# Prompt attention of a hybrid decoder step: turned weights ahead of the next scores, mask and maximum in one VectorE pass, alternating score banks, outputs turned in threes

## The reference, cut to what matters

```python
# branch A, group g: s = q_g . k * HEAD_DIM**-0.5, masked to its band; p = exp(s - m); l = sum(p)
o = jnp.einsum('nbhqk,nbkhd->nbqhd', p / l, vc)
lse = m + jnp.log(l)
# merged: alpha = softmax(lse over the 3 groups); out = sum_g alpha_g * o_g
# branch B: s masked to the selected keys, p = softmax(s), o = p @ v
```

## Time and profile before

| | us |
|---|---|
| median of 3 runs | 3498.6 |
| profiled execution | 3499.64 |
| its span | 3498.1 |
| prompt attention, first score product to the end of the last output copy | 2163.5 to 2583.9 |
| TensorE busy over the span | 3278.1 (94%) |
| VectorE / ScalarE / GpSimd busy | 1736.3 / 742.1 / 250.3 |

### The profile page before, as it was taken

How to read it: one execution, slowest core, us unless ns; L and a number is a source line. 1 busy time by engine, 2 the same in 40 slices (tenths; PEclk the granted TensorE clock), 3 DMA queues, 4 the chain that set the end, 5 groups by cost and what they waited for, 6 DMA issues and landing times.

```text
span 3498.1 us, 52866 instructions
## 1 busy us (share of the span) xinstructions
PE 3278.1 (94%) x20840; PEld 3042.7 (87%) x20840; DVE 1736.3 (50%) x2497; ACT 742.1 (21%) x1166; POOL 250.3 (7%) x393
## 2 busy tenths in 40 slices
PE   6888999999999999999999997888988899999997
PEld 4656999999999999999999996566665699999997
DVE  4554878710332455554555553654433364564654
ACT  4121000011001112111111112222222233433332
POOL 3000000000000000000000000211113201000000
PEclk7889999999999999999999998999998899999998
DMA  9722222222222222332333327412037667495672
GB/s 322 240 86 87 73 68 74 74 73 62 67 73 61 80 85 87 91 108 69 99 96 91 101 64 230 122 49 66 13 99 240 209 213 211 140 279 140 194 208 78
DMA packets 522864, 422.04 MB, mean 121 GB/s; under 512 B 19835, under 2 KB 491131, under 8 KB 519491
## 3 DMA queue, kind: packets, MB, share of 16 engines
q1 hardware_dynamic: 500044, 338.53, 33.9%
q0 software_dynamic: 22720, 82.20, 6.3%
HBM read 346.96 MB, written 75.81 MB: 121 GB/s over the span
## 4 chain that ended last, share of the span: by engine, by line
PE 86%; DVE 5%; DMA 4%; ACT 2%; issue 1%; SPq 1%; POOL 0%; DVEq 0%; POOLq 0%; ACTq 0%
PE banks L278 18%; PE banks L280 18%; PE banks L279 18%; PE banks L1451 6%; PE banks L1453 6%; PE banks L1452 6%; PE banks L651 4%; DVE mx L574 2%; DMA ada_w<-in_w_ada 1%; PE banks L680 1%; PE banks L670 1%; PE banks L654 1%; DMA u_raw<-in_w_out 1%; PE banks L333 1%; PE banks L1991 1%
## 5 line engine op out<-in xcount | busy, mean ns | idle before, releaser
L278 PE MATMUL banks<-h_hi,w_hi 128*128 128x352 f32 (+2 forms) x3744 | 1227.0, 328 | 12.2 <-DVE w_lo L269 10.1
L280 PE MATMUL banks<-h_hi,w_lo 128*128 128x352 f32 (+2 forms) x3744 | 1222.3, 326 | 0.0
L279 PE MATMUL banks<-h_lo,w_hi 128*128 128x352 f32 (+2 forms) x3744 | 1221.4, 326 | 0.0
L278 PEld LDWEIGHTS banks<-h_hi,w_hi 128*128 128x128 f32 (+1 forms) x3744 | 701.6, 187 | 17.0 <-issue 15.7
L279 PEld LDWEIGHTS banks<-h_lo,w_hi 128*128 128x128 f32 (+1 forms) x3744 | 704.0, 188 | 1.3
L280 PEld LDWEIGHTS banks<-h_hi,w_lo 128*128 128x128 f32 (+1 forms) x3744 | 700.8, 187 | 1.3
L269 DVE TENSOR_TENSOR w_lo<-w_raw,w_hi 128x2048 fp32r<-128x2048 f32 (+1 forms) x79 | 180.0, 2278 | 640.7 <-ACT w_hi L265 532.0
L1501 DVE MAX8 best<-work 128x8 f32<-128x1088 f32 x224 | 289.3, 1291 | 10.8 <-issue 1.0
L304 ACT ACTIVATE col<-banks 128x384 f32<-128x384 f32 x150 | 71.2, 475 | 1027.6 <-PE banks L280 1027.6
L1503 DVE MATCH_REPLACE8 work<-best,work 128x1088 f32<-128x1088 f32 x224 | 285.8, 1276 | 0.0
L265 ACT CAST w_hi<-w_raw 128x2048 fp32r<-128x2048 f32 (+1 forms) x79 | 149.8, 1896 | 582.9 <-PE banks L280 538.7
(11 more groups left out here) (237 smaller groups left out, 3359.9 us busy)
## 6 DMA issues: line engine op xcount, KB each, us to landing
w_raw<-in_w_in SPq DMA_DIRECT2D x78, 1024.0 KB, 5.7
u_raw<-in_w_out SPq DMA_DIRECT2D x96, 512.0 KB, 5.4
scratch_proj<-col POOLq DMA_DIRECT2D x78, 544.0 KB, 3.0
ada_w<-in_w_ada SPq DMA_DIRECT2D x16, 2048.0 KB, 13.8
u_raw<-in_w_pb SPq DMA_DIRECT2D x48, 512.0 KB, 4.7
gate_w<-in_w_ada SPq DMA_DIRECT2D x16, 1024.0 KB, 7.7
u_raw<-in_w_pa SPq DMA_DIRECT2D x48, 256.0 KB, 3.2
gates<-scratch_proj SPq DMA_DIRECT2D x64, 192.0 KB, 2.5
```

Source lines behind the costliest of these rows:

```text
L278: nc.tensor.matmul(dst, w_hi[:, par, k, 0:width], h_hi[:, k, a:b], start=(k == 0), stop=False)
L279: nc.tensor.matmul(dst, w_hi[:, par, k, 0:width], h_lo[:, k, a:b], start=False, stop=False)
L280: mm = nc.tensor.matmul(dst, w_lo[:, par, k, 0:width], h_hi[:, k, a:b], start=False, stop=(k == KT - 1))
```

## The change

In the scores of A jobs in rows 4 to 7 (16 jobs) and of B jobs in rows 2 to 7 (48 jobs), called `in_place`, TensorE no longer adds the mask. VectorE reads scores and bf16 mask, adds them, multiplies by -SCALE, writes the result back to the same PSUM columns and accumulates the minimum straight into `nmx`, in one instruction; the exp then uses scale -1. The other 32 jobs keep mask product, maximum and multiplication.

TensorE's step n becomes: half 0 of job n-2, every third step the outputs of the last complete triple, scores of job n, half 1 of job n-2, values of job n-3. VectorE's step n becomes: copy of half 0 of job n-2, output copies, mask and maximum of job n, reciprocal and scaling of job n-3. ScalarE copies half 1 of job n-2 ahead of the exp of job n. Score banks go by triples: (0-3, 4-5, 0-1), then (2-5, 0-1, 4-5), so that the scores of a job share banks with the job two before, never with the one before. The outputs of a triple are turned as soon as its three jobs are scaled, in the free columns of bank 7. GpSimd's sums are cut anew: in rows 0 to 3 as before; in rows 4 to 7 blocks i-4 to 3 first, then blocks 4 to i, then the two near blocks. From row 5 on, half 0 of an A job waits only for the first of them.

```diff
-        s_bank = lambda n: 0 if JOBS[n][0] == "A" else 4 + (JOBS[n][2] % 2 if JOBS[n][1] < 4 else 0)
+        s_bank = lambda n: ((0, 4, 0), (2, 0, 4))[n // 3 % 2][n % 3]
+        in_place = lambda n: JOBS[n][1] >= (4 if JOBS[n][0] == "A" else 2)
...
+        triple_due = lambda n: (n - 4) // 3 if n >= 4 and (n - 4) % 3 == 2 else None
+        def group_sums(n):
+            i = JOBS[n][1]
+            near = (i - 1 if i else 0, i + 1, (i + 1 + min(5, i + 1)))
+            if i < 4:
+                return [(0, i + 1, i + 1), near]
+            return [(i - 4, 4, i + 1), (4, i + 1, i + 1 + 8 - i), near]
...
-            for n in range(NJ + 5):
-                if n < NJ:
-                    dve.wait_ge(s_done, n + 1)
-                    nc.vector.tensor_reduce(mx[:, n:n + 1], flat(s_bank(n), P, width_of(n)), AX, ALU.max)\
-                        .then_inc(mx_set, 1)
+            for n in range(NJ + 4):
                 m = n - 2
                 if 0 <= m < NJ:
                     dve.wait_ge(t_done, use_no["w", m, 0] + 1)
                     need(dve, pv_done, m - 1)
                     w = min(4, blocks_of(m)) * P
                     nc.vector.tensor_copy(p_t[:, m % 2, 0:w], banks[:, T_BANK, 0:w]).then_inc(t_out, 1)
...
+                    dve.wait_ge(ot_done, x + 1)
+                    nc.vector.tensor_copy(o_t[:, i % 2, a, :], banks[:, O_BANK, P:2 * P])
+                    nc.vector.tensor_copy(o_t[:, i % 2, HA + 2 * a:HA + 2 * a + 2, :], ...).then_inc(ot_out, 1)
+                if n < NJ:
+                    if in_place(n):
+                        nc.vector.tensor_tensor_reduce(out=src, in0=src, in1=mask, scale=-SCALE, scalar=-TAKEN,
+                                                       op0=ALU.add, op1=ALU.min, accum_out=nmx[:, n:n + 1])\
+                            .then_inc(nmx_set, 1)
...
+                    early = half == 0 and JOBS[n][1] >= 5
+                    pe.wait_ge(groups_added, sums_before(n) + (1 if early else len(group_sums(n))))
...
+            def turn_outputs(x):
+                i, a = x // HA, x % HA
+                pe.wait_ge(o_out, 3 * x + 3)
+                for y, m in enumerate((a, HA + 2 * a, HA + 2 * a + 1)):
+                    tr = nc.tensor.transpose(banks[:, O_BANK, (y + 1) * P:(y + 2) * P],
+                                             o_tok[:, i % 2, m * P:(m + 1) * P], ident[:])
+                tr.then_inc(ot_done, 1)
...
-            for n in range(NJ + 5):
+            for n in range(NJ + 4):
+                if 2 <= n < NJ + 2:
+                    turn_weights(n - 2, 0)
+                if triple_due(n) is not None:
+                    turn_outputs(triple_due(n))
                 if n < NJ:
                     scores(n)
-                if 2 <= n < NJ + 2:
-                    turn_weights(n - 2, 0)
+                if ("w", n - 2, 1) in use_no:
+                    turn_weights(n - 2, 1)
                 if 3 <= n < NJ + 3:
                     values(n - 3)
```

More of the change, by code:

```diff
@@ L421, in decode_step @@
         width_of = lambda n: (sum(s[1] for s in SEG(JOBS[n][1])) if JOBS[n][0] == "A" else JOBS[n][1] + 1) * P
-        s_bank = lambda n: 0 if JOBS[n][0] == "A" else 4 + (JOBS[n][2] % 2 if JOBS[n][1] < 4 else 0)
+        s_bank = lambda n: ((0, 4, 0), (2, 0, 4))[n // 3 % 2][n % 3]
+        in_place = lambda n: JOBS[n][1] >= (4 if JOBS[n][0] == "A" else 2)
         s_banks = lambda n: set(range(s_bank(n), s_bank(n) + (width_of(n) + 511) // 512))
         exps_before = lambda n: max([m + 1 for m in range(n) if s_banks(m) & s_banks(n)], default=0)
-        a_jobs = lambda n: sum(JOBS[m][0] == "A" for m in range(n))
         T_BANK, O_BANK = 6, 7
         USES = []
-        for n in range(NJ + 5):
-            if 2 <= n < NJ + 2:
[L432 to L436, removed]
-        use_no = {u: x for x, u in enumerate(USES)}
+        for n in range(2, NJ + 2):
+            USES.append(("w", n - 2, 0))
+            if blocks_of(n - 2) > 4:
+                USES.append(("w", n - 2, 1))
+        use_no = {u: x for x, u in enumerate(USES)}
+        triple_due = lambda n: (n - 4) // 3 if n >= 4 and (n - 4) % 3 == 2 else None
[5 more added lines that the diff above has]
+            return [(i - 4, 4, i + 1), (4, i + 1, i + 1 + 8 - i), near]
+        sums_before = lambda n: sum(len(group_sums(m)) for m in range(n) if JOBS[m][0] == "A")
         def flat(bank, rows, width):
@@ L512, in act_attention @@
             nc.scalar.copy(mask_b[:], mask_f[:]).then_inc(mask_cast, 1)
-            for n in range(NJ + 5):
+            for n in range(NJ + 2):
+                m = n - 2
+                if ("w", m, 1) in use_no:
+                    act.wait_ge(t_done, use_no["w", m, 1] + 1)
+                    nc.scalar.copy(p_t[:, m % 2, 512:blocks_of(m) * P], banks[:, T_BANK, 0:(blocks_of(m) - 4) * P]).then_inc(t_out, 1)
                 if n < NJ:
@@ L517, in act_attention @@
                     nc.scalar.activation(p_buf[n % 3][:, 0:width_of(n)], flat(s_bank(n), P, width_of(n)), ACT.Exp,
[L518 to L523, removed]
+                                         bias=nmx[:, n:n + 1], scale=-1.0 if in_place(n) else SCALE,
+                                         accum_out=lsum[:, n:n + 1]).then_inc(exp_done, 1)
             act_sample(act)
@@ L543, in pool_attention @@
                     pool.wait_ge(exp_done, n + 1)
[L544 to L548, removed]
+                    done = sums_before(n)
+                    for first, end, src in group_sums(n):
+                        dst = p_buf[n % 3][:, first * P:end * P]
+                        if src > i + 1 and end == i + 1 and first >= i - 1:
+                            pool.wait_ge(groups_added, done)
+                        nc.gpsimd.tensor_tensor(dst, dst, p_buf[n % 3][:, src * P:(src + end - first) * P], ALU.add)\
                             .then_inc(groups_added, 1)
-                        off += w
-                        pool.wait_ge(groups_added, 2 * a_jobs(n) + seg_no(seg))
+                        done += 1
                 if n % PER == 0 and 2 <= i + 1 < QT:
@@ L594, in dve_attention @@
                                             None, ALU.mult).then_inc(o_out, 1)
[L595 to L601, removed]
             dve_sample(dve)
@@ L644, in scores @@
                 else:
-                    mask = keep_b[:, i % 2, 0:(i + 1) * P] if i >= 2 else None
-                    strips = [(q_tile[:, i % 2, GRP * HA + h, :], HA + h // (HB // KVB), 0, (i + 1) * P, mask)]
+                    strips = [(q_tile[:, i % 2, GRP * HA + h, :], HA + h // (HB // KVB), 0, (i + 1) * P, None)]
                 at_col = 0
```

47 lines of the change are left out of this document (32 added, 15 removed).

## The result

The changed kernel takes 3460.28 us in the median of four runs (3457.47 to 3465.28), the kernel before 3496.14 (3491.21 to 3506.04) beside it: ratio 0.9895, 95% interval 0.987 to 0.9921. That is 36 us less. Forecast were 3442 us, and 57 us less for the profiled execution, which measured 39 us less (3499.64 and 3460.39): the direction and the range (3422 to 3478) held, but only about two thirds of the forecast gain came.

The account below looks back on a forecast made before the run. TensorE was taken as neither free of waits nor the only bound: 318 of 418.2 us work, 100 waits and slower clock. Row sums gave 358.3, 59.9 less; 3 given back, so 57 off 3499.6: 3442 us, 80% range 3422 to 3478.

Parts of the forecast that it names:

- rows 5 to 7: Windows of these rows forecast at 48.4, 54.4 and 69.9 us, for 67.1, 73.6 and 90.4 before.
- The fused pass: VectorE's mask-and-minimum pass: priced at the maximum's 2.157 us for 1920 PSUM columns plus 0.1 us for the accumulator read.
- The Trainium skill's rule on two-source operations: VectorE's pass: spared by the rule's letter, 3442 us; if the rule held for it, 3470 us.
- The early order's wait: TensorE, rows 0 to 4: half 0 ahead of the scores leaves less cover, waits of 1.9 to 2.5 us a triple.
- I give 3 us back for a fall of the clock now and then: Rows 0 to 4: allowance for TensorE's clock falling in the new 2.4 us waits; gain 57 us instead of 59.9.
- Rival 3: TensorE's clock stays at its lower level in the 20 triples of rows 0 to 4: 88 us, 3530 us; chance 7%.
- A wait: TensorE's turning of an A job's weights waits for GpSimd's sums: 1.9 to 2.5 us a triple in rows 0 to 4.
- The outputs' wait: TensorE's output turning waits for the scaling of values computed just before: 0.2 to 0.5 us a triple, 10 us in all.
- rival 2: Early order costs more: each A wait 1 us longer, step signals not hidden, some 20 us more, 3462 us; chance 7%.
- the signs named ahead: Among them: clock 0.98 or more in rows 3 to 7, windows of rows 0 to 3 a little longer.
- the mask products: TensorE's mask additions: 32 us in the sum of the stage's work before, at 0.22 us per 512 columns.

Follow-up runs that it names:

- both: The kernel before with the fused pass and the outputs in threes, without the new order, banks or sums: 3450.37 us, ratio 0.9849.

## Why the prediction was right, and where not

**The direction and rows 5 to 7: right.** The prices from the earlier trace rows (0.11 a turned block, 0.224 a block of values, 0.86 per 512 score columns) gave 15.2 us for a triple of row 7, and 15.2 was measured. That the three rows meet their sum within 1 us is in part luck: row 7 was 2.4 us shorter than summed (0.9 in its first triple, the rest in the drain), and row 6 was 1.1 longer, through a wait of GpSimd's sums behind the mask's cast that was in no sum.

**The fused pass: right.** The nearest PSUM rows gave 2.157 + 0.1; it is 2.167 + 0.142.

**The Trainium skill's rule on two-source operations** (Vector Engine (DVE) Microarchitecture Reference, Points that are easy to get wrong), that two SBUF sources that aren't bf16 halve the throughput of its operation of this kind, spares this pass by its letter. The trace fits that: with one source in PSUM and one in bf16 the pass runs 1920 columns in 2.167 us, the maximum's own 2.157 plus 0.010. No run here has the case that the rule speaks of.

**The early order's wait: place right, size too large, its consequence under-sized.** A wait of 1.9 to 2.5 us in each triple of rows 0 to 4 was in the sum, 46.4 us; the trace has it 20 times, with 1.6 us on average, at most 2.7 and 31.8 in all. That error helped the forecast. The term that failed is "I give 3 us back for a fall of the clock now and then". It is at least 10.4 us in rows 1 to 4, as the run with added work shows. Rival 3 had the mechanism, but for every triple: the clock fell in one triple of four in row 1 and in two of four in rows 2 to 4.

**A wait that no sum had.** The prediction put a job's scaling right behind its values; on VectorE it stands behind the maximum of the next job. The values' wait for it takes 6.2 us in rows 0 to 3, half of it in row 1. Row 1's triple took 8.2 us at a clock of 1.00, not 7.7, although its A wait was 1.4 us and not 2.4. The outputs' wait for the same scaling, which was in the sum with at most 2.0 us a row, is 1.8 us in row 1 and 0.2 in row 3 (2.9 and 0.9 by the weight loads), so at most a small part of the surplus. So rival 2's direction is found in rows 1 and 2, 4.3 us with the clock at 1.00, but by another wait than it named: its A waits weren't longer, and at a clock of 1.00 rows 3 and 5 have no surcharge (11.4 and 12.2 us a triple for 11.4 and 12.1).

**The 21.2 us together:** 5.6 in row 0, at least 10.4 for the clock in rows 1 to 4, 5.2 for what is left in those rows. Of the signs named ahead, two failed: the clock was 0.93 and 0.94 in rows 3 and 4, not 0.98 or more, and rows 0 to 3 are 23.6 us longer than before, not a little. One sum is off without effect: the mask products come to 33.2 us at the prediction's price, not 32.

**What the sum couldn't tell:** it compared the whole change with the kernel before, row by row, and never priced the new order by itself. Its own numbers had it: 6.2 us lost in rows 0 to 3 although masks and output rounds also got cheaper there. Beside "both", the order (with its banks and sums) was a loss in five of eight rows, and net a loss of 10 us by the stage's windows.

**Open:** why two of four triples lose their clock and not all, and why row 0 is slower than forecast and than in "both" (25.6 against 21.2 us at clocks of 0.71 and 0.90). Its A waits are 3.7 us in all, and a clock of 0.93 did not shorten it. No run tested the values' wait by itself, for instance with the scaling ahead of the maximum: that it costs rows 1 and 2 their surplus is read from the trace and not shown by an experiment.

## What to carry to other kernels

Price a new order by itself, stretch by stretch: moving a dependent step ahead of the next independent one helps where the chain behind it is shorter than the cover, and hurts where it is longer; the same loop can need both orders. A wait of TensorE can cost its length and a slower clock behind it, as in rows 1 to 4 here; if work put into the wait makes the kernel faster, the clock cost at least that much. For every wait in the sum, list what else stands on the other engine ahead of the instruction that releases it: here a scaling behind another job's maximum. Before looking for an order that hides a copy, price the plain savings: fewer products and short, frequent output rounds gave 50 us, the order took 10 back.

## What the runs showed of the hardware

- VectorE reads a float32 PSUM operand and a bf16 one from SBUF, adds, scales, writes PSUM back and accumulates a minimum at the price of the maximum alone (2.167 against 2.157 us for 1920 columns); reading the accumulator takes another 0.142 us.
- 40 float32 products of 512 columns, whose result nobody reads, made the kernel 10 us faster: with an A wait of 1.4 to 2.7 us in every triple the granted clock was 0.90 to 0.94 in rows 1 to 4, with the products in them 1.00.
- With the turned outputs of before the granted clock is 0.95 in rows 5 to 7; with the outputs in threes and nothing else changed it is 1.00, and these rows are 21.2 us shorter (231.1 and 209.9). How much of this is the clock and how much the shorter rounds was not separated.
